# Two modulation blocks beside every pair of both networks' layers, and a second network over 516 instead of 528 tokens

## The reference, cut to what matters

```python
def conv_glu_ffn(x, w_up, conv_w, conv_b, w_down):
    u = x @ w_up
    ...                                   # depthwise, causal, width 3: token t reads t-2, t-1, t
    gate, val = jnp.split(u, 2, axis=-1)
    return (jax.nn.silu(gate) * val) @ w_down

# first block, for each of its 2 layers
    h = h + mix_out
    h = h + conv_glu_ffn(rms_norm(h, norm_ffn_g[layer]), ...)
return rms_norm(h, final_norm_g)[:, N_META:, :]      # N_META = 16

# second block, for each of its 2 layers
def adaln(cvec, w, b):
    m = (jax.nn.silu(cvec) @ w + b)[..., None, :]    # w: 1024 x 6144
    return jnp.split(m, 6, axis=-1)
```

## Time and profile before

| what | value |
|---|---|
| time, median of 3 runs | 3179.85 us (3176.12 to 3186.61) |
| the profiled execution's own time | 3173.93 us |
| its span | 3172.1 us |
| PE busy | 3044.1 us, 96% |
| DVE busy | 1755.7 us, 55% |
| ACT busy | 1303.1 us, 41% |
| POOL busy | 541.6 us, 17% |

### The profile page before, as it was taken

One profiled execution on the slowest core, in us unless ns is written; L12 is line 12 of the kernel. 1 busy time (PEld: TensorE's weight loads), 2 busy tenths in 40 slices (PEclk: granted clock), 3 DMA queues, 4 the chain that ended last, 5 costly groups with the idle time before them and its releaser, 6 DMA issues.

```text
span 3172.1 us, 46617 instructions
## 1 busy us (share of the span) xinstructions
PE 3044.1 (96%) x19340; PEld 2675.3 (84%) x19340; DVE 1755.7 (55%) x2648; ACT 1303.1 (41%) x2229; POOL 541.6 (17%) x530
## 2 busy tenths in 40 slices
PE   6999999999999999999999979899999999999998
PEld 6987878789999999999999977666788878878887
DVE  7675545546666553545666675553654543355353
ACT  4464555433323363654323335443432332243231
POOL 0002222122213100002212322221110211122020
PEclk9899999999999999999999999999999999999999
DMA  3210000024554522013455441101223222222232
GB/s 108 74 49 34 1 1 1 35 87 133 168 189 134 189 83 74 1 44 124 134 195 168 150 161 67 40 1 53 80 95 97 92 84 98 93 80 96 92 96 82
DMA packets 79506, 284.32 MB, mean 90 GB/s; under 512 B 8480, under 2 KB 9248, under 8 KB 78528
## 3 DMA queue, kind: packets, MB, share of 16 engines
q1 hardware_dynamic: 79296, 281.35, 26.7%
HBM read 274.96 MB, written 6.36 MB: 89 GB/s over the span
## 4 chain that ended last, share of the span: by engine, by line
PE 86%; DVE 7%; DMA 3%; ACT 3%; issue 1%; POOL 0%; SPq 0%; DVEq 0%; ACTq 0%; POOLq 0%
PE psum L345 57%; DMA araw<-d_ada 3%; PE psum L1193 2%; PE psum L2598 2%; PE psum L839 2%; PE psum L1783 2%; PE psum L1214 2%; PE psum L1980 1%; PE psum L1225 1%; DVE wlo L302 1%; DVE araw L426 1%; PE psum L1222 1%; PE psum L1962 1%; PE psum L1953 1%; PE psum L782 1%
## 5 line engine op out<-in xcount | busy, mean ns | idle before, releaser
L302 DVE TENSOR_TENSOR wlo<-wraw,whi 128x1024 fp32r<-128x1024 f32 (+2 forms) x398 | 500.1, 1282 | 640.5 <-ACT whi L295 639.1
L295 ACT CAST whi<-wraw 128x1024 fp32r<-128x1024 f32 (+2 forms) x398 | 395.9, 1021 | 513.4 <-PE psum L345 481.6
L426 DVE CUSTOM_DVE_ANT_0 araw<-araw,cond 128x1024 f32<-128x1024 f32 x112 | 137.3, 1236 | 83.5 <-DMA araw<-d_ada 83.2
L345 PE MATMUL psum<-f0xh,whi 128*128 128x264 f32 x704 | 144.1, 286 | 7.9 <-DVE wlo L302 4.0
L345 PE MATMUL psum<-f1xh,whi 128*128 128x264 f32 x704 | 143.8, 286 | 5.5 <-DVE f1xl L540 3.9
L345 PE MATMUL psum<-f2xh,whi 128*128 128x512 f32 x352 | 140.3, 399 | 4.2 <-DVE f2xl L536 4.2
L345 PE MATMUL psum<-f3xh,whi 128*128 128x512 f32 x352 | 140.0, 398 | 4.2 <-DVE f3xl L536 4.2
L345 PE MATMUL psum<-f1xh,wlo 128*128 128x264 f32 x704 | 143.7, 286 | 0.0
L345 PE MATMUL psum<-f0xh,wlo 128*128 128x264 f32 x704 | 143.6, 286 | 0.0
L345 PE MATMUL psum<-f1xl,whi 128*128 128x264 f32 x704 | 143.3, 285 | 0.0
L345 PE MATMUL psum<-f0xl,whi 128*128 128x264 f32 x704 | 143.1, 285 | 0.0
(11 more groups left out here) (511 smaller groups left out, 8617.3 us busy)
## 6 DMA issues: line engine op xcount, KB each, us to landing
wraw<-d_w SPq DMA_DIRECT2D x357, 512.0 KB, 3.4
araw<-d_ada SPq DMA_DIRECT2D x112, 512.0 KB, 3.3
wraw<-d_w SPq DMA_DIRECT2D x32, 384.0 KB, 3.1
hn<-d_h SPq DMA_DIRECT2D x4, 528.0 KB, 7.7
hres<-d_h SPq DMA_DIRECT2D x1, 2112.0 KB, 8.2
spill<-hres SPq DMA_DIRECT2D x1, 2112.0 KB, 7.4
hres<-spill SPq DMA_DIRECT2D x1, 2112.0 KB, 8.6
cond<-d_cond SPq DMA_DIRECT2D x2, 1024.0 KB, 4.8
```

What stands on the lines that cost most here:

```text
L295: e.copy(whi[0:rows, n % NH, 0:kt * cols], wraw[0:rows, n % NR, 0:kt * cols]).then_inc(*w_hi.up(n))
L302: e.tensor_tensor(wlo[0:rows, n % NH, 0:kt * cols], wraw[0:rows, n % NR, 0:kt * cols], whi[0:rows, n % NH, 0:kt * cols].bitcast(F32), ALU. ...
L345: ins = e.matmul(psum[0:bw, b0 + nb * len(sl) + si, 0:ln], l_ if z == 2 else h_, (xp.lo if z == 1 else xp.hi)[:, k, o:o + ln], start=k == ...
L426: e.tensor_tensor_reduce(out=w, in0=w, in1=self.c[:, col, :], scale=1.0, scalar=0.0, op0=ALU.mult, op1=ALU.add, accum_out=ada[:, ly, blk, ...
```

## The change

Two edits. First, DVE takes 2 modulation blocks after every up pair and 2 ahead of every down pair's additions, where it took 1 and 5, in F0 and in F1. The count of blocks stays 54 and 58. Second, sbo and F1 run over tokens 12 to 527 (516 of them) and not over 0 to 527: the causal convolution of width 3 reaches two tokens back from token 16, so tokens 0 to 11 are never read again. Every matmul of these two stages has 258 columns and not 264, and every elementwise operation on their activations 516 and not 528. The other stages are the same.

```diff
                     if F.ada:
-                        F.ada.dve(e, 1)
+                        F.ada.dve(e, 2)
...
                     if F.ada:
-                        F.ada.dve(e, 5)
+                        F.ada.dve(e, 2)
...
-        F1 = Ffn("f1", hres1, L, True, 1)
-        sq_f1 = Squares("f1", lambda k: hres1[:, k, :], F1.sq, lambda e, k: e.wait_ge(*res.at("sbo", k)))
+        T1 = 12
+        LT = L - T1
+        h1 = hres1[:, :, T1:L]
+        F1 = Ffn("f1", h1, LT, True, 1)
+        sq_f1 = Squares("f1", lambda k: h1[:, k, :], F1.sq, lambda e, k: e.wait_ge(*res.at("sbo", k)))
...
-            lin_pe(e, "sbo", XoT, 4, L, lambda e, k: None, room)
+            lin_pe(e, "sbo", XoT, 4, LT, lambda e, k: None, room, parts=[(XoT, T1 + o, ln) for o, ln in splits(LT)])
...
-            add_dve(e, "sbo", "sbo", hres1, L)
+            add_dve(e, "sbo", "sbo", h1, LT)
```

## The result

The changed kernel takes 3152.44 us in the median of 6 runs (3139.77 to 3158.61), the kernel before 3178.97 us beside it (6 runs, 3171.18 to 3186.61). The ratio is 0.991, with a 95% interval of 0.9894 to 0.9926: 26.5 us less, where 38.9 were forecast. The time lies in the range of 3132 to 3157, 11 us above the 3141 forecast, and the number alone would fit rival A (3151) and rival B (3152) better than the forecast; it takes the profile to tell them apart. The profiled execution of after took 3158.34 us, the longest but one of its six, with a span of 3156.4 us and a mean granted clock of 0.973.

The account below looks back on a forecast made before the run. PE, busy 96% of the span, was taken to bound the kernel, with stalls in down parts; 29 (blocks) + 9.6 (columns) + 0.3 (F1's serial start) = 38.9 us off 3179.85 gives 3141 us, range 3132 to 3157.

Parts of the forecast that it names:

- rival A: Matmuls of sbo and F1: fewer columns give nothing, since the weight load sets the pace; 3151 us, chance 0.10.
- rival B: Up pairs: DVE keeps POOL out over both blocks, so later steps overrun; 3147 to 3158 us, middle 3152, chance 0.15.
- Part 1: Down parts of F0 and F1: 2 and 2 blocks remove waits for modulation loads; sum 30.0 us, taken as 29.
- the last addition: F1's tail: no block is left in the last pair to hold the last residual addition; 1.2 us saved.
- ACT's squares: F1's last down part: ACT squares the residual before making `whi`, so a late addition delays weights; excess there 17.2 us.
- The second block at no cost: 44 up pairs: POOL gets in between DVE's two blocks; 0.4 of 1.27 us slack used, cost zero.
- Rival C: Up pairs: the second block's load lands late and PE waits; at 14 us loads 3220 us, chance 0.03.
- Part 2: sbo and F1: 516 tokens take 6 columns off each of 3552 matmuls; 2.7 ns each, 9.6 us.
- the price of a column: sbo and F1 matmuls: 0.45 ns per column, from 512 against 264 columns; bounds none and 0.62 ns, 13.2 us.
- rows that begin at other multiples of bytes: F1's input: rows begin at multiples of 16 bytes, second part at 8, before 32; taken as no effect.
- the signs named: Profile after: F1 down halves 62 to 63 us, F0's 63.5 to 64, F1 pace 0.1188 us, full clock, no up-part `wlo` waits.
- The offset of the runs: Whole kernel: median of runs stays 5.9 us above the profiled execution, as before; 5 us allowed at the low end.

Follow-up runs that it names:

- a third block: The changed kernel with 3 modulation blocks after an up pair instead of 2: 3162.55 us, ratio 0.9951 to the kernel before.
- the streams: Matmuls on PE alone in the kernel's loop order, nothing else computed, with columns and row layout varied: 111.5 ns at 128 columns, 226.8 at 512.
- the second set: The changed kernel run again, unchanged, against the kernel before: 3142.1 us (5 runs), ratio 0.9874.

## Why the prediction was right, and where it was off

**What bounds the kernel: right.** The time went where the excess over the undisturbed pace lay, and nowhere else.

**Part 1, 29 us: right in mechanism and in size.** Blocks alone gave 29.1 us, 6.2 in F0, where 6.3 were read, and 22.3 in F1, where 22.9 less 0.4 were forecast. The reading of excess from the earlier trace rows was good to a few tenths. Only the last addition, priced at 1.2 us, gave 0.6. Why F1 lost more than F0 was told in part. In the 66 us of its last down part PE stood still for 11.7 us (busy 54.3) and the lower clock cost some 5 us (66 x 0.08). The prediction put the standing still to ACT's squares, which delay `whi` and so `wlo`; half of it, 5.9 us, was PE's own wait for the residual addition at the matmul of the context's sum, which it had not named. Both waits hang on the same late addition, and both are gone with it, as is the low clock (1.00 after). How the rest divides between the squares and the loads was not tried.

**The second block at no cost: right.** Turn-taking priced it (2.31 us where 2.3 to 2.5 were forecast, POOL 2.15). Rival B, with 3.3 us for POOL, falls. The Trainium skill (SBUF — State Buffer, "Who interferes with whom") says that such instructions exclude each other; the order in which they get in was the part that only the trace could give. Rival C falls too: loads landed in a median of 3.2 and at most 6.5 us, and DVE never waited for one. The price of a third block, 15.6 us in two networks, shows that there was room for one and not for two; the third also waited for its own load, so the slack and the two buffers are not told apart.

**Part 2, 9.6 us: too large.** The term that was mis-sized is the price of a column, 0.45 ns. It is right as a mean slope from 248 to 272 columns (0.44) and about right from 264 to 512 (0.424 in the streams). It was applied to six columns, where the layout moves the pace by half as much as they do and more. Measured were 1.4 ns per matmul, 0.24 ns a column: 3168 x 1.4 = 4.4 us in F1, and the traces have 4.0 (388.3 - 384.3). In sbo the first and last starts lie 45.6 us apart instead of 46.6, 1.0 us, with what surrounds the matmuls in it. The matmuls are worth 1.4 x 3552 = 5.0 us, not 9.6, and the traces have the same 5.0. The lines at one clock put the whole part at 7.5 to 7.8 us (3154.9 - 3147.4 and 3177.5 - 3169.7, each good to 1.8), which leaves a rest of some 2.5 us beside the matmuls, little more than these bounds, that I can't place. The prediction had named this gap, rows that begin at other multiples of bytes, and set it at nothing, while each ns was 3.6 us. Against the slope of 0.45 the pace with 258 columns is 1.3 ns too slow, and 1.3 x 3.6 = 4.7 us is what is missing; the bounds of 0 and 13.2 us hold the 5.0. The remark that no row had a column as cheap as 1/2.4 ns was a slip: the row of 118.6 ns gives 0.40. Of the signs named, the down halves of F1 at 62 to 63 us (63.1 and 63.5) and the pace of 0.1188 (0.1201) missed by this term. The others came, but for one wait of PE for `wlo` in the first 20 us of each network, 1.7 us in F0 and 0.7 in F1. Rival A, columns that give nothing, isn't true either: the floor of 111.5 ns is reached only at 224 columns.

**The offset of the runs: a step that the sum did not hold.** The forecast assumed that a run of after would lie as far from its trace as one of before. The clock that the code ahead of F0 gets moves a run by up to 18 us, and a set's median by 10: 3152, 3142 and 3152 for one kernel. Of the 11 us between 3141 and 3152.4, 38.9 - 34 = 5 are the columns' and 6 are this. Over all 17 runs of after the median is 3148.9, over the 44 of before 3180.1: 31 us. In the second set the same kernel took 3142.1 us, next to the forecast although the columns' term was 5 us too large: how near a set's median comes to 3141 is in part luck with this clock. What sets the clock in that code and in the stretch between F0 and F1 was not tried and stays open.

**A version that beats both** is 520 tokens with two and two blocks: F1 takes 381.4 and 381.5 us in its two traces against 384.3 in three of after, and at one clock it is 2.7 us faster (3144.7 ± 1.1 against 3147.4 ± 0.9). The medians alone, 3142.4 and 3144.0 against 3142.1 to 3152.4, would not have told it.

## What to carry to other kernels

Read a stall's cost from the first and last start of the matmuls of a tile against the undisturbed pace, not from the sum of waits: that gave 29 where 29.1 were measured, the clock's part included. Spread side work over every pair to the depth that its buffers and the engines' idle time allow, and count the turns that two engines take at each other, not only their own durations. For a gain under 1%, compare segments of traces or times at one granted clock, since the medians of the same kernel differed by 10 us; and before trimming a few columns, time that very layout, since its neighbour may be faster.

## What was not expected of the hardware

With the weights reloaded for each matmul of 128 rows and 128 columns of weights, the pace is flat at 111.5 ns up to 224 columns and 0.417 ns a column from 320 to 512. In between, at an equal count of columns, the length of the row and the place of its second part move it by up to 2.3 ns (119.0 to 121.3 at 260). And the same code at the same busy share was granted a clock of 0.83 in one execution and 0.95 in another (400 to 500 us); the whole kernel's time follows the mean clock with 2.36 us per 0.001 between 0.970 and 0.983.
